# Gate and up matmuls over both halves of X at once: one 512-column matmul in place of two of 256

## The reference

```python
def swiglu(h, w_gate, w_up, w_down):
    return (jax.nn.silu(h @ w_gate) * (h @ w_up)) @ w_down
...
x = x + 0.5 * swiglu(rmsnorm(x, norm_g[layer, 0]), ffn_w_gate[layer, 0], ffn_w_up[layer, 0], ffn_w_down[layer, 0])
```

## Time and profile before

| | us |
|---|---|
| Time, median of 3 runs (lowest, highest) | 2700.56 (2699.87, 2701.85) |
| Profiled execution, its time | 2699.39 |
| Profiled execution, span from first to last instruction | 2697.6 |
| PE busy | 2657.3 |
| DVE busy | 1687.4 |
| ACT busy | 1407.1 |
| POOL busy | 266.4 |

### The profile page before, as it was taken

The page is one execution under the profiler, slowest core; times in us unless marked ns, Lnnn a source line. Parts: engine busy times, 40 slices in busy tenths (PEclk is TensorE's granted clock), DMA queues, the critical chain, the costliest instruction groups (busy, mean ns, idle before and its releaser), DMA issues.

```text
span 2697.6 us, 40286 instructions
## 1 busy us (share of the span) xinstructions
PE 2657.3 (99%) x17348; PEld 2400.0 (89%) x17348; DVE 1687.4 (63%) x2031; ACT 1407.1 (52%) x1790; POOL 266.4 (10%) x246
## 2 busy tenths in 40 slices
PE   9999999999999999999999999999999999999999
PEld 8998779999987779999998888899999988888998
DVE  5567765555557765555568587655555586876554
ACT  5446655345446655444457567444443575674443
POOL 0004110000005010000013023100000031131000
PEclk9999999999999999999999999999999999999999
DMA  7655445555555455555555364555555553645553
GB/s 248 193 169 175 146 164 179 184 183 188 187 169 172 144 169 188 186 174 188 188 171 166 108 209 159 182 186 187 173 188 188 175 167 118 199 161 173 187 188 125
DMA packets 342767, 472.18 MB, mean 175 GB/s; under 512 B 18811, under 2 KB 259517, under 8 KB 342589
## 3 DMA queue, kind: packets, MB, share of 16 engines
q1 hardware_dynamic: 342588, 469.61, 53.9%
HBM read 468.46 MB, written 1.11 MB: 174 GB/s over the span
## 4 chain that ended last, share of the span: by engine, by line
PE 87%; DVE 7%; ACT 4%; issue 1%; POOL 0%; DMA 0%; SPq 0%; DVEq 0%; ACTq 0%
PE PS L99 84%; DVE WL L108 3%; PE PS L102 2%; ACT WH L105 2%; DVE XB L116 1%; DVE RL L116 1%; POOL XB L108 0%; ACT RH L105 0%; ACT SB L105 0%; DVE SB L119 0%; ACT L105 0%; DMA ST<-in_w_in 0%; DVE ZR L116 0%; DVE TZ L108 0%; DVE MG L116 0%
## 5 line engine op out<-in xcount | busy, mean ns | idle before, releaser
L108 DVE TENSOR_TENSOR WL<-ST,WH 128x2048 fp32r<-128x2048 f32 (+3 forms) x442 | 1012.4, 2291 | 546.8 <-ACT WH L105 546.4
L105 ACT ACTIVATE WH<-ST 128x2048 fp32r<-128x2048 f32 (+3 forms) x442 | 831.3, 1882 | 718.7 <-PE PS L99 709.0
L99 PE MATMUL PS<-XH,WH 128*128 128x256 f32 x3456 | 983.6, 285 | 1.5 <-DVE XL L116 1.5
L99 PE MATMUL PS<-XL,WH 128*128 128x256 f32 x3456 | 978.3, 283 | 0.0
L99 PE MATMUL PS<-XH,WL 128*128 128x256 f32 x3456 | 978.3, 283 | 0.0
L99 PEld LDWEIGHTS PS<-XH,WH 128*128 128x128 f32 x3456 | 663.3, 192 | 7.0 <-issue 2.3
L99 PEld LDWEIGHTS PS<-XL,WH 128*128 128x128 f32 x3456 | 663.6, 192 | 3.8 <-issue 1.0
L99 PEld LDWEIGHTS PS<-XH,WL 128*128 128x128 f32 x3456 | 663.3, 192 | 0.0
L99 PE MATMUL PS<-WH,RH 128*128 128x512 f32 (+1 forms) x1056 | 411.1, 389 | 14.0 <-DVE QB L113 6.1
L99 PE MATMUL PS<-WL,RH 128*128 128x512 f32 (+1 forms) x1056 | 408.4, 387 | 0.0
L99 PE MATMUL PS<-WH,RL 128*128 128x512 f32 (+1 forms) x1056 | 407.6, 386 | 0.0
(11 more groups left out here) (235 smaller groups left out, 1926.4 us busy)
## 6 DMA issues: line engine op xcount, KB each, us to landing
ST<-in_ffn_w SPq DMA_DIRECT2D x132, 1024.0 KB, 5.0
ST<-in_w_in SPq DMA_DIRECT2D x106, 1024.0 KB, 5.2
ST<-in_ffn_w_down SPq DMA_DIRECT2D x44, 1024.0 KB, 4.9
ST<-in_ffn_w_gate SPq DMA_DIRECT2D x43, 1024.0 KB, 5.3
ST<-in_ffn_w_up SPq DMA_DIRECT2D x43, 1024.0 KB, 5.3
ST<-in_w_ssd_out SPq DMA_DIRECT2D x16, 1024.0 KB, 5.0
ST<-in_w_branch SPq DMA_DIRECT2D x8, 1024.0 KB, 5.0
ST<-in_w_out SPq DMA_DIRECT2D x8, 1024.0 KB, 5.0
```

Of the source, the lines that this page charges most:

```text
L99: return self.eng.matmul(o, l, r, start=start, stop=stop) if self.eng else Said()
L105: return self.eng.activation(o, v, f, **kw) if self.eng else Said()
L108: return self.eng.tensor_tensor(o, a, b, op) if self.eng else Said()
```

## The change

`XH` and `XL` become the two halves of one tensor `XHL` [128, 8, 2, 256], so that for each k the 256 columns of `XH` and those of `XL` lie side by side. A gate or up tile now does, for each k: two matmuls of 512 columns (`WH` of column half f = 0, then f = 1, by `XH` and `XL` together), then two of 256 columns (`WL` of f = 0, then f = 1, by `XH`). The high-by-low product lands in columns 256 to 511 of the bank, apart from the other two. Gate has banks 4 and 5 for every pair, up has 6 and 7. ACT copies columns 256 to 511 of both banks to SBUF (`GB`, `UB`), and DVE adds columns 0 to 255 to it into `GS` or `US`; with that the banks are free. The later steps (row factor, Silu, product) then read `GS` and `US` in SBUF.

```diff
--- before.py
+++ after.py
@@ -30,6 +30,7 @@
     FFN += [("g", _i), ("u", _i), ("d", _i - 2)]
 FFN += [("d", NP - 2), ("d", NP - 1)]
 UP_AT = {i: FFN.index(("u", i)) for i in range(NP)}
+GATE_AT = {i: FFN.index(("g", i)) for i in range(NP)}
 MIX2 = [("xbc", 0), ("xbc", 1), ("xbc", 2), ("uq", 0), ("uq", 1), ("uq", 2), ("ukv", 0), ("ukv", 1), ("uq", 3),
         ("xbc", 3), ("gate2", 0), ("xbc", 4), ("xbc", 5), ("gate2", 1), ("xbc", 6), ("xbc", 7), ("xbc", 8),
         ("xbc", 9), ("mla", 0), ("xbc", 10), ("xbc", 11), ("mla", 1), ("z", 0), ("z", 1), ("z", 2), ("gate1", 0),
@@ -349,8 +350,8 @@
     ST = sb("ST", [128, NS, 2048], F32)
     WH = sb("WH", [128, NR, 2048], F32R)
     WL = sb("WL", [128, NR, 2048], F32R)
-    XH = sb("XH", [128, 8, T], F32R)
-    XL = sb("XL", [128, 8, T], F32R)
+    XHL = sb("XHL", [128, 8, 2, T], F32R)
+    XH, XL = XHL[:, :, 0, :], XHL[:, :, 1, :]
     X = sb("X", [128, 2, DM], F32)
     R2 = where[0]
     RH = sb("RH", [128, 16, T], F32R)
@@ -388,6 +389,7 @@
     ANG = [ar("ANG0", [128, 3, 2, 8], 28736), ar("ANG1", [128, 3, 2, 32], 28992)]
 
     GS, US = ar("GS", [128, 2, 2, T], 2048), ar("US", [128, 2, 2, T], 2048 + 4096)
+    GB, UB = ar("GB", [128, 2, T], 32768), ar("UB", [128, 2, T], 32768 + 2048)
     HB = RH[:, :, :].rearrange("p (a b) t -> p a b t", b=2)
     HL = RL[:, :, :].rearrange("p (a b) t -> p a b t", b=2)
 
@@ -687,9 +689,8 @@
                 if last:
                     e.also("tile", tile)
                 continue
-            which, b = what == "u", 4 + 2 * (i % 2)
-            if not which:
-                clear(b, b + 1)
+            b = 4 + 2 * (what == "u")
+            clear(b, b + 1)
             for k in range(8):
                 if s == 0 and k == 3:
                     turn_x(e, p, "", 1)
@@ -698,13 +699,11 @@
                 if s == 0:
                     e.wait_ge(*at("xl", p, "", k))
                 for f in range(2):
-                    o, fs = PS[:, b + f, which * 256:which * 256 + 256], of(f)
-                    e.matmul(o, wh[:, k, fs], XH[:, k, :], k == 0, False)
-                    e.matmul(o, wh[:, k, fs], XL[:, k, :], False, False)
-                    m = e.matmul(o, wl[:, k, fs], XH[:, k, :], False, k == 7)
+                    e.matmul(PS[:, b + f, :], wh[:, k, of(f)], XHL[:, k, :, :].rearrange("p a t -> p (a t)"), k == 0, False)
+                for f in range(2):
+                    m = e.matmul(PS[:, b + f, 0:256], wl[:, k, of(f)], XH[:, k, :], False, k == 7)
             m.then_inc(*e.done("tile", tile))
-            if which:
-                freed[b] = freed[b + 1] = ("m", p, i)
+            freed[b] = freed[b + 1] = ("us" if what == "u" else "gs", p, i)
             if s == 2:
                 r_row(e, p, 3)
 
@@ -1168,6 +1167,17 @@
                     if i >= 4:
                         e.wait_ge(*at("tile", t0 + FFN.index(("d", i - 4))))
                     e.activation(HB[:, i % 4], US[:, i % 2], ACT.Copy).then_inc(*e.done("hh", p, i))
+            for i in range(NP):
+                if s == UP_AT[i] + 1:
+                    e.wait_ge(*at("tile", t0 + UP_AT[i]))
+                    if i:
+                        e.wait_ge(*at("us", p, i - 1))
+                    e.activation(UB[:, :, :], PS[:, 6:8, 256:512], ACT.Copy).then_inc(*e.done("ub", p, i))
+                if s == GATE_AT[i] + 1:
+                    e.wait_ge(*at("tile", t0 + GATE_AT[i]))
+                    if i:
+                        e.wait_ge(*at("gs", p, i - 1))
+                    e.activation(GB[:, :, :], PS[:, 4:6, 256:512], ACT.Copy).then_inc(*e.done("gb", p, i))
             if s == 0 and p == 0:
                 split_x_hi(e, p, "", 1)
                 for j in range(CUT[1]):
@@ -1610,11 +1620,17 @@
                                     ALU.subtract).then_inc(*e.done("hl", p, i))
             for i in range(NP):
                 if s == max(UP_AT[i] + 1, 3):
-                    b = 4 + 2 * (i % 2)
-                    e.wait_ge(*at("tile", t0 + UP_AT[i]))
                     e.wait_ge(*e.last())
-                    e.tensor_tensor(GS[:, i % 2], PS[:, b:b + 2, 0:256], RBC[:, :].unsqueeze(1).to_broadcast([128, 2, T]),
+                    e.tensor_tensor(GS[:, i % 2], GS[:, i % 2], RBC[:, :].unsqueeze(1).to_broadcast([128, 2, T]),
                                     ALU.mult).then_inc(*e.done("gg", p, i))
+                if s == UP_AT[i] + 1:
+                    e.wait_ge(*at("ub", p, i))
+                    e.wait_ge(*e.last())
+                    e.tensor_tensor(US[:, i % 2], PS[:, 6:8, 0:256], UB[:, :, :], ALU.add).then_inc(*e.done("us", p, i))
+                if s == GATE_AT[i] + 1:
+                    e.wait_ge(*at("gb", p, i))
+                    e.wait_ge(*e.last())
+                    e.tensor_tensor(GS[:, i % 2], PS[:, 4:6, 0:256], GB[:, :, :], ALU.add).then_inc(*e.done("gs", p, i))
             if s == 0:
                 split_x_lo(e, p, "", 1)
             if s == 0 and p == 0:
@@ -1627,10 +1643,9 @@
                 row_end(e, p, 3)
             for i in range(NP):
                 if s == max(UP_AT[i] + 1, 3):
-                    b = 4 + 2 * (i % 2)
                     e.wait_ge(*at("silu", p, i))
                     e.wait_ge(*e.last())
-                    e.tensor_tensor(US[:, i % 2], GS[:, i % 2], PS[:, b:b + 2, 256:512], ALU.mult).then_inc(*e.done("m", p, i))
+                    e.tensor_tensor(US[:, i % 2], GS[:, i % 2], US[:, i % 2], ALU.mult).then_inc(*e.done("m", p, i))
             if p == 0 and s == 22:
                 vector_tables(e)
             if p == 0 and s == 26:
```

## The result

The changed kernel takes 2670.53 us (median of 4 runs, 2668.79 to 2671.90), the kernel before 2700.78 beside it: the ratio is 0.9887, with an interval from 0.9871 to 0.9903. The forecast was 2669.5, faster, in a range from 2662 to 2687. The profiled execution took 2670.72 us; its span is 2668.9.

The account below looks back on a forecast made before the run. The prediction took PE's dense matmul stream in the FFNs as the bound: 2699.4 - 33.5 (matmuls) + 2.4 (wait in the first FFN) = 2668.3 us, with the median of runs 1.2 higher: 2669.5, range 2662 to 2687.

Parts of the forecast that it names:

- TensorE's term: Gate and up tiles: 719.4 to 695.6 ns per k, 0.190 us less per tile, 33.5 us less over 176 tiles.
- 0.228, 0.228, 0.120, 0.120 apart: Expected trace sign: within a k of a gate or up tile, matmul starts about this many us apart.
- the sign of 11.13 per pair: Expected trace sign: a gate and up pair between two down tiles takes 11.13 us instead of 11.51.
- ACT and DVE: Steady blocks: added copies and additions put about 0.65 us into a chain with 6 us of cover, so no PE wait.
- The start: First FFN: gate 1 waits 2.4 us (bounds 0 and 3) for banks 4 and 5; later FFNs don't wait.
- The sum: Profiled execution: 2699.4 - 33.5 + 2.4 = 2668.3 us; median forecast 2669.5, 1.15% less.
- the wait for the second half of X: Tile 0 of each FFN: PE may wait up to 0.1 us at k = 4, under 1 us over all, left out.
- Alternation slow: Rival, gate and up tiles: long matmuls stay at 235 ns each, total 2689.5 down to 2675.4 us; chance 14%.
- Nothing removed: Rival, gate and up tiles: a long matmul costs exactly two short ones, total 2703 us; length-free part not removed, chance 5%.
- small fixed part of 2.5 ns: Rival, gate and up tiles: each instruction fewer saves only 2.5 ns, 7.0 us in all, total 2696.0 us.
- Price per change: Rival, gate and up tiles: each change from short to long costs 27 ns, total 2704 us; chance 6%.
- Stall in every FFN: Rival, FFN starts: gate 1 waits 2.4 us in all eight FFNs, 19.2 us, total 2686 us; chance 3%.

Follow-up runs that it names:

- short matmuls in the new frame: Against the changed kernel, each long matmul split again into two of 256 columns, with banks, copies and additions kept: 2702.05 us, ratio 1.0008.
- early copy: Against the changed kernel, the ACT copy of gate 0 put ahead of the norm's sums of squares, first FFN only: 2668.05 us, ratio 0.9883.
- grouped order: Against the changed kernel, all 16 long matmuls before the 16 short ones in every tile but an FFN's first: 2669.57 us, ratio 0.9885.

## Why the prediction was right

*TensorE's term.* 11.13 us per pair were forecast from 227.9 and 119.9 ns per matmul, 11.13 or 11.14 were measured in 64 of 64 steady blocks. The short matmuls in the new frame show that nothing else contributes. But the value taken was right by luck. The long matmuls stand at 232.5 and 233.0 ns, 5 more each than the mean of a down tile that I took, and the short ones at 114.7 and 115.8, 4 to 5 less each: two errors that cancel to 0.4 ns per k. The sign "0.228, 0.228, 0.120, 0.120 apart" did not come; the sign of 11.13 per pair did. What I hadn't counted is that the down tiles gain 0.016 us each: 72 x 0.016 = 1.2 us more. (The block stands eight times in each FFN, not nine; the sum doesn't use it.)

*ACT and DVE.* The copies cost 0.60 (bounds 0.61 to 0.7 from the nearest rows, so just outside), the additions 0.69 as read. A block has 10.33 us of DVE, as worked out, and 7.75 of ACT (8.04 worked out). `WL` behind the up tile ended 0.1 us earlier than worked out, at 70.0 against 68.1 + 2.02; the product ran 0.3 later. PE has no wait in the steady state, and with 3 us more per tile only three, for `WL`, in all eight FFNs.

*The start.* Gate 1 was forecast to lose 2.4 us and started 2.41 late, from the place named: gb(0) behind the sums of squares on ACT. The later FFNs had no wait, as forecast; in the third gs(0) ended at 610.8 and gate 1 started at about 613.5. What is wrong is the size of this term: I let the clock be, and in the profiled execution 1.65 us of low clock came behind the wait, in the second profile of the same kernel none. With the early copy neither was there.

*The sum* for the profiled execution was 31.1 us less, 28.7 were measured. 176 x 0.188 + 1.2 = 34.3 come from matmuls, and PE got its first data 0.7 earlier. Against it stand 2.4 and 1.65 at gate 1, and 1.5 in the second mixer, where a wait that both kernels have was followed by low clock in one only (below). That is 29.4. Of the 0.7 that are left, 0.6 stand in tile 0, which gained only 0.05 to 0.18 us per FFN and not 0.19. That may be the wait for the second half of X, which the prediction had named and left out. By medians it is 30.25 against 31.1 forecast.

*The rivals.* "Alternation slow" was largely right in its mechanism: the long matmuls stay slow, at 233 ns against its 235, and the short ones behind them give time back, 9 ns per k against its "up to 10". It was too low by 23.4 - 19.6 = 3.8 ns per k, since 235 is 2 ns too much for each long one; the forecast's own mechanism, long ones at the mean of a down tile, is not what the trace shows, though its sum is. "Nothing removed" and the small fixed part of 2.5 ns fell with the pair at 11.13: 16 instructions fewer saved 0.19 us per tile, 11.7 ns each. "Price per change" of 24.5 ns and more fell with the grouped order. "Stall in every FFN" didn't come. With 3 us more on ACT it came in six of the eight FFNs, but short; the larger waits then stood at up 2, which the prediction doesn't look at.

## What to carry to other kernels

In a dense stream the price of a matmul is its distance to the next start, and here it has a part that doesn't depend on the columns: one of 512 columns took 227 ns, two of 256 took 240. Two operands that share a stationary one were worth laying side by side, even though another 200 us of copies and additions came onto engines that had room. Look for that room where it is thinnest, at the start and the end of each stage, and not in the steady state. When long and short matmuls are mixed, try the order: strict alternation cost 13 us here, while sixteen and sixteen against two and two can't be told apart by their times. And check a forecast by its parts: this one's total came out although both distances in it were off.

## What was not expected of the hardware

**The order of long and short matmuls has a price**, with the same columns and the same loads: steady pairs of 11.105 us (16 and 16), 11.135 (2 and 2), 11.29 (1 and 1). But the same strict alternation ran at two rates in one execution, 5.55 and 5.65 us per tile, and why is open.

**A wait of about 1.8 us may or may not bring the low clock.** At gate 1 of the first FFN the waits were 1.22, 1.27, 1.35 and 1.83 us with gate 1 at full clock after it, and 1.82 and 2.25 with it low; 1.83 and 2.25 are two executions of the same kernel. A wait of 1.74 us in each of the two mixers, the same in all kernels, shows the same. The first window is the second mixer of the kernel before, the second that of the changed one, both from the first matmul after the wait; the column behind the engines is the granted clock.

```profile
873.17:878.00 4.83, 4.83 (x25) 3.83 (x26) 4.19 (x12) 4.80 (x9) 4.67 (x3) 1.00 0.48 184
```

```profile
863.98:869.00 5.02, 5.02 (x19) 3.66 (x20) 4.35 (x12) 4.99 (x11) 4.86 (x3) 0.66 0.44 171
```

From that wait to the next one behind it the mixer takes 85.1 us with the clock held and 86.6 with it low, and once, in the second profile of the changed kernel, 88.1. So it costs 1.5 us, at gate 1 1.65, and once 3.0, which may be a good part of the 3 us by which executions of one kernel differ here. The Trainium skill ("TensorE: Matmul & The Clock Gate", Part 1: The HAM clock gate) says that the clock is set by how busy the engine has recently been and that the moment of change varies from run to run; that one place comes out either way here agrees with it.
